# Two more units of a feed-forward projection as block products, with GpSimd making two of four weight sums

## What is computed

```
def sq_relu_mlp(xn, w_in, w_out):
    h = jax.nn.relu(xn @ w_in)
    return (h * h) @ w_out

h = h + sq_relu_mlp(rms_norm(h, norm_mlp_g[i]), mlp_w_in[i], mlp_w_out[i])     # for both layers i
```

## Time and profile before

| | us |
|---|---|
| median of three runs | 1874.09 |
| lowest and highest | 1874.01, 1874.39 |
| the profiled execution | 1874.33 |
| its span in the profile | 1872.5 |
| TensorE busy | 1860.4 |
| VectorE busy | 1259.4 |
| ScalarE busy | 904.9 |
| GpSimd busy | 101.9 |

### The profile page before, as it was taken

The page is one execution under the profiler, slowest core; times in us unless marked ns, Lnnn a source line. Parts: engine busy times, 40 slices in busy tenths (PEclk is TensorE's granted clock), DMA queues, the critical chain, the costliest instruction groups (busy, mean ns, idle before and its releaser), DMA issues.

```text
span 1872.5 us, 27658 instructions
## 1 busy us (share of the span) xinstructions
PE 1860.4 (99%) x10387; PEld 1537.4 (82%) x10387; DVE 1259.4 (67%) x1744; ACT 904.9 (48%) x1158; POOL 101.9 (5%) x90
## 2 busy tenths in 40 slices
PE   9999999999999999999999999999999999999998
PEld 7788878888888877877889898988778788989897
DVE  7757774677357667556577675847788658758484
ACT  6392464555133344544444443545667744435262
POOL 0010021000000021000100000020110010000001
PEclk9999999999999999999999999999999999999999
DMA  6223122322322235222332323234232133232321
GB/s 242 90 89 123 40 68 68 112 90 68 112 90 98 75 97 145 68 70 68 101 101 91 107 83 109 91 110 147 87 105 72 60 102 103 82 110 90 105 91 68
DMA packets 146795, 179.23 MB, mean 96 GB/s; under 512 B 3581, under 2 KB 140669, under 8 KB 144256
## 3 DMA queue, kind: packets, MB, share of 16 engines
q1 hardware_dynamic: 143296, 160.44, 26.5%
q0 software_dynamic: 3104, 17.10, 2.9%
q10 hardware_dynamic: 288, 0.26, 0.0%
HBM read 173.48 MB, written 2.20 MB: 94 GB/s over the span
## 4 chain that ended last, share of the span: by engine, by line
PE 96%; DVE 2%; ACT 1%; issue 0%; DMA 0%; ACTq 0%; DVEq 0%
PE bank L1015 24%; PE bank L1013 24%; PE bank L1014 24%; PE bank L1417 4%; PE bank L1419 4%; PE bank L1418 4%; PE bank L1141 2%; PE bank L1717 1%; PE bank L1699 1%; PE bank L1147 1%; PE bank L1588 1%; PE bank L1590 1%; PE bank L1589 1%; PE bank L1523 1%; PE bank L1576 1%; PE bank L1200 0%
## 5 line engine op out<-in xcount | busy, mean ns | idle before, releaser
L1807 ACT ACTIVATE w_hi<-raw 128x2048 fp32r<-128x2048 f32 (+2 forms) x121 | 226.5, 1872 | 422.7 <-PE bank L1015 420.3
L1013 PE MATMUL bank<-n_hi,w_hi 128*128 128x512 f32 x1054 | 424.7, 403 | 1.3 <-DVE w_lo L1813 1.3
L1015 PE MATMUL bank<-n_hi,w_lo 128*128 128x512 f32 x1054 | 418.1, 397 | 0.0
L1014 PE MATMUL bank<-n_lo,w_hi 128*128 128x512 f32 x1054 | 416.6, 395 | 0.0
L1813 DVE TENSOR_TENSOR w_lo<-raw,w_hi 128x2048 fp32r<-128x2048 f32 (+2 forms) x127 | 284.9, 2243 | 155.1 <-ACT w_hi L1807 153.3
L1014 PE MATMUL bank<-ff_lo,w_hi 128*128 128x512 f32 x848 | 334.5, 394 | 0.0
L1015 PE MATMUL bank<-ff_hi,w_lo 128*128 128x512 f32 x784 | 312.5, 399 | 0.0
L1013 PE MATMUL bank<-ff_hi,w_hi 128*128 128x512 f32 x784 | 307.8, 393 | 0.0
L1013 PEld LDWEIGHTS bank<-n_hi,w_hi 128*128 128x128 f32 x1054 | 198.0, 188 | 54.3 <-issue 5.0
L1014 PEld LDWEIGHTS bank<-n_lo,w_hi 128*128 128x128 f32 x1054 | 198.0, 188 | 49.1 <-issue 2.9
L1015 PEld LDWEIGHTS bank<-n_hi,w_lo 128*128 128x128 f32 x1054 | 197.9, 188 | 46.4
(11 more groups left out here) (429 smaller groups left out, 2788.3 us busy)
## 6 DMA issues: line engine op xcount, KB each, us to landing
raw<-in_mlp_w_in SPq DMA_DIRECT2D x32, 1024.0 KB, 5.4
raw<-in_mlp_w_out SPq DMA_DIRECT2D x32, 1024.0 KB, 5.1
raw<-in_w_up SPq DMA_DIRECT2D x22, 1024.0 KB, 5.1
raw<-in_w_units SPq DMA_DIRECT2D x14, 1024.0 KB, 4.8
raw<-in_a_w_qkv SPq DMA_DIRECT2D x12, 1024.0 KB, 5.2
raw<-in_b_w_qkv SPq DMA_DIRECT2D x12, 1024.0 KB, 5.2
b_bias<-bias_table POOLq DMA_DIRECT2D x16, 448.0 KB, 4.6
raw<-in_w_down SPq DMA_DIRECT2D x8, 768.0 KB, 4.6
```

The lines of the kernel that those rows point to most:

```text
L1013: nc.tensor.matmul(b[:, :], w_hi[:, j % 2, cols], hi, start=start, stop=False)
L1014: nc.tensor.matmul(b[:, :], w_hi[:, j % 2, cols], lo, start=False, stop=False)
L1015: return nc.tensor.matmul(b[:, :], w_lo[:, j % 2, cols], hi, start=False, stop=final)
L1807: act.activation(w_hi[:, s, cols], raw[:, s, cols], ACT.Copy).then_inc(hi_ready, 1)
```

## The change

- In quarters 1 and 2 of each layer (`has_down`) the third and fourth units of the second projection become block units 4 and 5. The first two stay plain (`begun_down_tensor`).
- Their T factors are sums over the squared activations and differ in each quarter: `down_sums` makes four on VectorE, `t_split_high` and `t_split_low` split them. For this the four units' results stay whole in `scratch`, and the kept rows move to a place of their own.
- `second_sum` and `fourth_sum` of every block unit, in bursts and projections, move from VectorE to GpSimd (`weight_sums`), behind a semaphore `sums_pool`. `piece_low` of A22 on VectorE waits for the fourth sum, which reads the raw weights.
- Results of units 4 and 5 are added to `hT` by `first_added`, `third_added`, `second_added` and `last_added` on VectorE.
- Blocks take alternate row tiles (`near_far`) as their two halves, before the first and the last four.
- Pieces have fixed places in `w_hi` and `w_lo`, A22 two of them in turn; before, the places rotated.
- The two orders by hand follow: `down_scalar` and `down_vector` run from the burst into block units 4 and 5 and from these into the next burst, whose unit 0 is prepared beside block unit 5.

The diff, cut to its core:

```diff
+        def near_far(v):
+            return v[:, 0:KD:2, :], v[:, 1:KD:2, :]
+
+        T_PLACE = {"T1": (0, EARLY), "T3": (0, LATER), "T4": (1, EARLY), "T2": (1, LATER)}
+
+        def t_whole(v, name):
+
+            far, cols = T_PLACE[name]
+            return near_far(v)[far][:, :, cols]
+
+        def t_high(name):
+            return {"T1": near_far(ff_hi)[0][:, :, LATER], "T2": t_mid[:, 0:4, :], "T3": t_mid[:, 4:8, :], "T4": t_far[:, :, :]}[name]
+
+        def down_operand(name):
+
+            if name[0] == "T":
+                return t_high(name), t_whole(scratch_r, name)
+            return [operand(v, None, name) for v in (ff_hi, ff_lo)]
...
-        PLACE = [1, 2, 3, 4, 5, 6, 7] + [0, 1, 2, 3, 4, 5, 6] + [0, 1, 7, 2, 3, 4, 5] + [0, 1, 2, 6, 7, 4, 5]
+        PLACE = {"A11": 0, "A12": 1, "A22": 2, "S2": 4, "S3": 5, "S1": 6, "S4": 7}
...
+        def has_down(m):
+            return m % 4 in (1, 2)
...
+        def block_before(m, u):
+
+            if u == FIRST_DOWN or (u == 0 and m % 4 == 1):
+                return None
+            return (m, u - 1) if u else (m - 1, BLOCKS - 1)
         def places_free(eng, m, op, u):
-            for piece in PIECE_OF_OP[op]:
-                n = PIECE_AT[piece, u]
-                before = [i for i in range(n) if PLACE[i] == PLACE[n]]
-                if before:
-                    eng.wait_ge(at("piece_used"), burst_of(m) * COUNTED + before[-1] + 1)
-                else:
-                    eng.wait_ge(w_used, p_in[m].u0 - (1 if PLACE[n] < 4 else 0))
+            before = block_before(m, u)
+            if before is None:
+                eng.wait_ge(w_used, unit_index(m, u) - (1 if op[0] == "A" else 0))
+            elif op != "A22":
+                piece_used(eng, before[0], (PIECE_OF_OP[op][-1], before[1]))
...
+        def second_sum(pool, m, u):
+            done(pool, pool.tensor_tensor(by_rows(sum_piece("S2", u)), by_rows(sum_piece("S1", u)), raw_piece(m, "A11", u), ALU.subtract),
+                 at("sums_pool"), pool_count(m, u, 2))
+
+        def fourth_sum(pool, m, u):
+            done(pool, pool.tensor_tensor(by_rows(sum_piece("S4", u)), raw_piece(m, "A12", u), by_rows(sum_piece("S2", u)), ALU.add),
+                 at("sums_pool"), pool_count(m, u, 3))
+
+        def weight_sums(pool, layer):
+            for m in range(4 * layer + 1, 4 * layer + 4):
+                for u in range(BLOCKS if has_down(m) else UNITS):
+                    pool.wait_ge(at("sums_ready"), sums_before(m) + SUM_AT[u] + 1)
+                    second_sum(pool, m, u)
+                    fourth_sum(pool, m, u)
...
+            weight_sums(pool, 0)
...
+                if has_down(m):
+                    begun_down_tensor(pe, m)
+                    for u in range(FIRST_DOWN, BLOCKS):
+                        block_tensor(pe, m, u)
+                else:
+                    project(pe, p_dn[m], FF_HI, FF_LO, pairs_ready=(ff_lo_ready, FF_BEFORE + 4 * m, 2))
+
...
+        def block_tensor(pe, m, u):
+            x, y, z, w = unit_banks(u)
+            g = unit_group(m, u)
+            pe.wait_ge(bank_free, g + 1)
+            piece_split(pe, m, "A1", u, "lo")
+            piece_product(pe, m, ("A11", u), x[:, EARLY])
+            piece_product(pe, m, ("A12", u), y[:, EARLY])
+            if block_before(m, u) is None:
+                pe.wait_ge(bank_free, g + 2)
+            piece_split(pe, m, "A22", u, "lo")
+            piece_product(pe, m, ("A22", u), z[:, EARLY])
+            piece_split(pe, m, "S23", u, "lo")
+            piece_product(pe, m, ("S2", u), y[:, LATER])
+            piece_product(pe, m, ("S3", u), w[:, EARLY])
+            piece_split(pe, m, "S14", u, "lo")
+            piece_product(pe, m, ("S1", u), z[:, LATER])
+            kept(pe, m, u)
+            piece_product(pe, m, ("S4", u), x[:, LATER])
+
         def burst_tensor(pe, m):
...
+            if op == "A22":
+                dve.wait_ge(at("sums_pool"), pool_count(m, u, 3))
+            ins = dve.tensor_tensor(by_rows(places(w_lo_flat, op, u), op), source(m, op, u), by_rows(places(w_hi_flat, op, u), op).bitcast(F32), ALU.subtract)
...
+            if u == 1 and has_down(m - 1):
+                piece_used(dve, m - 1, ("S3", BLOCKS - 1))
+            v, s = raw[:, unit_index(m, u) % 2, :], s_parts[u % 2 if u < UNITS else 0]
...
-        def second_sum(dve, m, u):
-            done(dve, dve.tensor_tensor(by_rows(sum_piece("S2", u)), by_rows(sum_piece("S1", u)), raw_piece(m, "A11", u), ALU.subtract),
-                 at("sums_ready"), sums_before(m) + 3 * u + 2)
-
-        def fourth_sum(dve, m, u):
-            done(dve, dve.tensor_tensor(by_rows(sum_piece("S4", u)), raw_piece(m, "A12", u), by_rows(sum_piece("S2", u)), ALU.add),
-                 at("sums_ready"), sums_before(m) + 3 * u + 3)
+            done(dve, dve.tensor_tensor(to, a, b, ALU.subtract), at("sums_ready"), sums_before(m) + SUM_AT[u] + 1)
...
+        def first_added(dve, m, u):
+
+            row, y = down_rows(u)[0], unit_banks(u)[1]
+            kept(dve, m, u)
+            piece_used(dve, m, ("S2", u))
+            own_dve(dve, dve.tensor_tensor(third_row(u), y[:, LATER], first_row(u), ALU.add))
+            own_dve(dve, dve.tensor_tensor(row, y[:, :], row, ALU.add))
+            own_dve(dve, dve.tensor_tensor(halves(row), halves(row), twice(first_row(u)), ALU.add))
+
+        def third_added(dve, m, u):
+            piece_used(dve, m, ("S3", u))
+            own_dve(dve, dve.tensor_tensor(third_row(u), unit_banks(u)[3][:, EARLY], third_row(u), ALU.add))
+
+        def second_added(dve, m, u):
+            piece_used(dve, m, ("S1", u))
+            row, below = down_rows(u)
+            z = unit_banks(u)[2]
+            own_dve(dve, dve.tensor_tensor(row[:, LATER], z[:, LATER], row[:, LATER], ALU.add))
+            own_dve(dve, dve.tensor_tensor(below, z[:, :], below, ALU.add))
+            own_dve(dve, dve.tensor_tensor(halves(below), halves(below), twice(third_row(u)), ALU.add))
+
+        def last_added(dve, m, u):
+            piece_used(dve, m, ("S4", u))
+            row = down_rows(u)[0][:, LATER]
+            done(dve, dve.tensor_tensor(row, unit_banks(u)[0][:, LATER], row, ALU.add), bank_free, unit_group(m, u) + 3)
+
+        def down_sums(dve, m):
+
+            n0 = sums_before(m) + UNITS + 1
+            t1, t3, t2, t4 = (t_whole(scratch, name) for name in T_SUMS)
+            done(dve, dve.tensor_tensor(t1, t3, t1, ALU.subtract), at("sums_ready"), n0 + 1)
+            done(dve, dve.scalar_tensor_tensor(t3, t2, -1.0, t3, ALU.mult, ALU.subtract), at("sums_ready"), n0 + 2)
+            done(dve, dve.scalar_tensor_tensor(t2, t2, -1.0, t1, ALU.mult, ALU.subtract), at("sums_ready"), n0 + 3)
+            done(dve, dve.tensor_tensor(t4, t2, t4, ALU.add), at("sums_ready"), n0 + 4)
+
...
+        def t_split_high(act, m, name):
+
+            act.wait_ge(at("sums_ready"), sums_before(m) + UNITS + 1 + len(T_SUMS))
+            if name == "T1":
+                act.wait_ge(w_used, p_dn[m].u0 + 2)
+            else:
+                piece_split(act, m, "S14", UNITS - 1, "lo")
+            ins = act.activation(t_high(name), t_whole(scratch, name), ACT.Copy)
+            ins.then_inc(at("piece_hi"), 1)
+            piece_split(act, m, name, FIRST_DOWN, "hi")
+
...
+        def down_scalar(act, m):
+            t_split_high(act, m, "T4")
+            t_split_high(act, m, "T2")
+            piece_high(act, m, "A1", FIRST_DOWN)
+            t_split_high(act, m, "T3")
+            piece_high(act, m, "A22", FIRST_DOWN)
+            piece_high(act, m, "S23", FIRST_DOWN)
+            t_split_high(act, m, "T1")
+            piece_high(act, m, "S14", FIRST_DOWN)
+            for u in range(FIRST_DOWN, BLOCKS):
+                first_kept(act, m, u)
+                for op in PIECE_OF_OP:
+                    if u + 1 < BLOCKS:
+                        piece_high(act, m, op, u + 1)
+                    else:
+                        piece_high(act, m + 1, op, 0)
+
...
+        def down_vector(dve, m):
+            ph = p_dn[m]
+            down_sums(dve, m)
+            t_split_low(dve, m, "T4")
+            t_split_low(dve, m, "T2")
+            residual_group(dve, ph, 0, 0)
+            piece_low(dve, m, "A1", FIRST_DOWN)
+            t_split_low(dve, m, "T3")
+            piece_low(dve, m, "A22", FIRST_DOWN)
+            residual_group(dve, ph, 0, 1)
+            piece_low(dve, m, "S23", FIRST_DOWN)
+            t_split_low(dve, m, "T1")
+            piece_low(dve, m, "S14", FIRST_DOWN)
+            for u in range(FIRST_DOWN, BLOCKS):
+                after = (m, u + 1) if u + 1 < BLOCKS else (m + 1, 0)
+                paired_sums(dve, *after)
+                piece_low(dve, after[0], "A1", after[1])
+                first_added(dve, m, u)
+                piece_low(dve, after[0], "A22", after[1])
+                third_added(dve, m, u)
+                piece_low(dve, after[0], "S23", after[1])
+                second_added(dve, m, u)
```

(30 more changed lines are left out.)

195 lines of the change are left out of this document (100 added, 95 removed).

## The result

The changed kernel takes **1895.76 us** (median of four runs, 1895.35 to 1896.77) against 1874.14 us for the kernel before, run beside it on the same chip: 1.0115 of its time, with a 95% interval of 1.0103 to 1.0127. The forecast was 1899.0 us in a range of 1886 to 1915, slower. The profiled execution took 1896.77 us with a span of 1894.9 us, 22.4 us more than before; the forecast for the difference was 24.9 us.

The account below looks back on a forecast made before the run. TensorE was taken to bound the kernel, with VectorE a near second. Changed quarters with their bursts 5.97 and 6.47 us longer make 12.44 a layer, 24.9 in all: 1899.0 us by the median, range 1886 to 1915.

Parts of the forecast that it names:

- first changed quarter and its burst: Second projection with two blocks plus the burst behind it: 91.09 us where it used to need 85.12, so 5.97 us longer.
- What TensorE saves: Eight units become block units of 10.08 us in place of 11.20: 8 x 1.12 = 8.96 us less on TensorE.
- Exclusion: VectorE splits and paired sums with two SBUF inputs shut out GpSimd's sums, which end 1.15 us after the release.
- How much comes back as waiting: In a VectorE turn, of the 1.46 us of sums moved to GpSimd, 1.4 us return as waiting.
- The second sum: GpSimd's second weight sum of a turn takes 1.30 us, running 3.73 to 5.03 us after the paired sum's start.
- The paired sum of block 4: VectorE's paired sum for the projection's first block waits 5.1 us for weights and runs 4.74 to 5.97 us after projection start.
- What was taken at nothing: ScalarE's T splits and high parts, fixed piece places, SyncE's loads and GpSimd's queue order were all assumed to cost nothing.
- TensorE's waits: TensorE waits for VectorE's low parts of A22, S23 and S14, some 17 us a layer; none in each layer's first burst.
- No exclusion: GpSimd's sums run beside VectorE's splits unhindered, most drift is absorbed, and the kernel takes 1871.6 us; chance 0.10.
- Sums that fit beneath other work: GpSimd's sums fit beneath A1 low and the first taking, 0.7 us each, so the saving arrives: about 1866 us; chance 0.07.
- Slow sums of 1.6 us: GpSimd's sums on strided operands take near 1.6 us each, giving 1914 us; chance 0.12.
- A fallen clock: The granted clock falls to the 1.2 GHz level when TensorE begins to wait, giving 1940 us; chance 0.03.

## Why the prediction was right, step by step

The forecast was right in sign, in mechanism and, within 3.2 us, in size. Most steps held. Two errors cancelled in the first quarter: that 91.09 us was met to 0.01 us there is luck, as the second quarter shows.

| step | forecast | measured |
|---|---|---|
| GpSimd's first sum, shut out | ends 1.15 after the split | 1.15 |
| GpSimd's second sum | 1.30 | 1.09 |
| turns, from the paired sum of block 5, first quarter | 11.72, 11.72, 10.48, 11.74 | 11.56, 11.56, 10.28, 11.56 |
| paired sum of block 5, from the projection's start | 30.56 | 31.45 |
| from the burst's last paired sum to the next projection | 14.86 | 14.67 |
| first changed quarter and its burst | 91.09 | 91.08 |
| second | 91.59 | 90.36 |
| a layer | +12.44 | +11.20 and +10.61 |
| the whole span | +24.9 | +22.4 |

**What TensorE saves, 8.96 us.** Right within 0.7 us: the four stretches of the kernel with the new order are 8.2 us shorter.

**Exclusion.** Right, and shown by the fills. The price of 1.15 us behind the release, from a row of GpSimd's work in another layer, was met to the hundredth for the first sum. One reading beside it was off and entered no sum: the held VectorE operation that finished 0.55 us behind the release had not all its work before it, since 512 elements take 0.69 us.

**How much comes back as waiting.** I wrote that of the 1.46 us moved away 1.4 come back. My own sum says more: a turn of 12.15 us less ScalarE's 0.87 and the 1.46 leaves 9.82 us of work, so a turn of 11.74 has 1.9 us of waiting. Measured were 1.73. So in a turn of the burst more came back than was moved. The forecast used the 11.74, not the 1.4.

**The second sum was mis-sized,** 1.29 us of the earlier trace rows where it takes 1.09 undisturbed. That row's inputs were whole tiles, and I took the number of elements to be all that counts. The exchanged inputs show that it isn't: with the piece of `raw` second, the same sum takes 1.29. That kernel's 1901.02 us is close to my 1899, which had assumed just that. The turns came out 0.16 to 0.20 us shorter for it, and the last piece of the stretch by as much (14.67 for 14.86).

**The paired sum of block 4 was late.** I had it 4.74 us from the projection's start, with 5.1 us for its weights. In the first changed quarter of the kernel after it came at 6.18. The issue of its load on SyncE's queue, then VectorE, then GpSimd:

```profile
1045.66 0.37 SPq L900 DMA_DIRECT2D raw<-in_mlp_w_out  x1
```
```profile
1052.11 1.23 DVE L2103 TENSOR_TENSOR consts<-raw 128x1024 f32<-128x1024 f32 x1 [3.26 <-DMA raw<-in_mlp_w_out]
...
1054.63 3.26 DVE L1914 TENSOR_TENSOR w_lo<-raw,w_hi 128x2048 fp32r<-128x2048 f32 x1
1057.92 2.00 DVE L2174 TENSOR_TENSOR scratch<-scratch 128x1024 f32<-128x1024 f32 x1
```
```profile
1055.82 3.02 POOL L1044 TENSOR_TENSOR consts<-raw,consts 128x512 f32<-128x512 f32 x1
```

From issue to use are 6.45 us; that load took 6.4. GpSimd's fourth sum fell beside the split of 1054.63 and was not over before 1058.84; the first of the four operand sums, which I had at 1.23 us, was held and took 2.00. The operand sums ended at 17.77 us from the start in place of 16.83, and this 0.9 us is the error at the paired sum of block 5. The shorter turns (0.7 us) and the shorter last piece (0.2 us) paid it back: 91.08 for 91.09. In the second changed quarter the paired sum came at 5.21 us, no operand sum was held, and the shorter turns show: 90.36 for 91.59. In the first stretch of layer 2 the paired sum came at 5.58 us and an operand sum again took 2.00, so the held sum is not a matter of this one load alone. The mean of a load should not have stood for this one. Why it was slow was not tried.

**What was taken at nothing.** Everything outside the four stretches came to 0.6 us: 0.4 of it lies ahead of the first projection (1045.93 for 1045.53 in the earlier trace rows), no more than this start differs between the kernels here. That ScalarE's high parts come in time was right for the four stretches of the kernel after, where no low part of a weight piece waited for one. It was not right in general: in the first burst A22's low part waited 1.51 us for ScalarE, at no cost, and with GpSimd's wait gone ScalarE is the next to be late, by 0.87 us.

**TensorE's waits.** Forecast some 17 us a layer; 91.08 + 90.36 less twice 82.88 is 15.7. Most of them lie where they were put, in front of pieces whose low part is late. TensorE's row at such a place in the kernel after:

```profile
1129.51 0.28 PE L1515 MATMUL bank<-ff_hi,w_lo 128*128 128x256 f32 x1
1131.01 0.39 PE L1513 MATMUL bank<-ff_hi,w_hi 128*128 128x256 f32 x1 [1.22 <-DVE w_lo L2083]
```

**The rivals.** No exclusion: forecast 1871.6, and the kernel with fills took 1872.61, so the rival was well priced and only its premise false. Sums that fit beneath other work: they did not, at 2.27 us for the first. The rival's 1866 was the price of a kernel that gets the whole saving, and 1865.5 was measured once the wait is moved and the order changed. Slow sums of 1.6 us: not so, at 1.29 and 1.09 us alone. A fallen clock: not so; the clock stayed at 1.00 though TensorE stood still for up to 1.4 us (from 1129.51 to 1131.01 in the rows above, where products start 0.12 us apart). The reason that I had not written down is that VectorE would be too slow even without GpSimd: 1893.2 with all sums on VectorE. The expectation of the reordered kernel was 2 us too high, and the one with the wait moved 3 us; what these 3 us are is open, since no run takes ScalarE's wait in that kernel away.

## What to carry to other kernels

An engine that is overloaded in one stage may catch up in the next. Before filling that next stage, add up its order of work in turns and compare a turn with the pace of the engine that bounds the kernel: once there is no time to catch up, each tenth of a microsecond per turn is paid in full. Work handed to a helper engine relieves the giver only if the giver doesn't wait for it: put the wait on whoever truly needs the result (here the queue of the load), and let the helper run beside operations that read banks. Before moving work, compare the wait that comes back with the work that goes: here 1.73 us came for 1.46 in a turn of the burst. After taking one wait away, look at what is next in line, since two waits that cover one another each seem worth little alone.

## What the runs showed of the hardware

- GpSimd's sum of 512 elements takes 1.29 us with the strided piece of `raw` as its second input and 1.09 us with it as its first. Why was not tried.
- A sum that is shut out ends 1.15 us after VectorE's release if it takes 1.29 alone (S2), and 0.95 us after it if it takes 1.09 (S4, in the kernel with one sum each). So it gets in at once, also between two VectorE operations 0.03 us apart: the sum of 1055.82 got in between the split that ended at 1057.89 and the operand sum of 1057.92.
- Whoever is held ends some 0.14 us sooner behind the release than its whole time alone: 1.15 for 1.29 and 0.95 for 1.09 us on GpSimd, 0.55 for 0.69 (the A22 split of 1110.96, behind GpSimd's end at 1111.69) and 1.08 for 1.23 us (the operand sum of 1057.92) on VectorE.
- A GpSimd fill of 1024 elements (0.96 us) beside a VectorE split of two SBUF inputs (1.23 us) lengthens neither; a GpSimd sum beside it is held until the split is over.
- When each waits for the other in turn, the delay is handed on: in one chain a split of 3.26 us (2.29 undisturbed), a GpSimd sum of 3.02 us (1.09) and a VectorE sum of 2.00 us (1.23) are each longer than alone.
